# One layer with top-1 group, top-2 expert routing: expert weights with eight rows a partition, 2 MB requests, and router edits

## The reference

```python
x2 = x + g1 * rmsnorm(mixed)                      # residual after token mixing
h  = rmsnorm(x2, pre_ffn_gain) * (1 + sc2) + sh2
gl = h @ w_group + b_group                        # top-1 group, softmax probability
el = h @ w_expert + b_expert                      # top-2 experts inside that group
gates = one_hot(e_idx) * g_w * tv                 # 256 x 32, two nonzeros a row
for wg, wu, wd, gt in experts:                    # 1024x512, 1024x512, 512x1024
    hid = silu(h @ wg) * (h @ wu)
    out += gt[:, None] * (hid @ wd)
```

## Time and profile before

| | us |
|---|---|
| median of three runs | 647.47 |
| the profiled execution's own time | 648.19 |
| its span, first to last instruction | 646.5 |
| TensorE busy in the span | 613.5 (95%) |
| DMA moved | 248.71 MB, 385 GB/s over the span |

### The profile page before, as it was taken

One profiled execution on the slowest core, in us unless ns is written; L12 is line 12 of the kernel. 1 busy time (PEld: TensorE's weight loads), 2 busy tenths in 40 slices (PEclk: granted clock), 3 DMA queues, 4 the chain that ended last, 5 costly groups with the idle time before them and its releaser, 6 DMA issues.

```text
span 646.5 us, 8690 instructions
## 1 busy us (share of the span) xinstructions
PE 613.5 (95%) x3445; PEld 321.9 (50%) x3447; DVE 168.3 (26%) x317; ACT 143.4 (22%) x335; POOL 73.7 (11%) x161
## 2 busy tenths in 40 slices
PE   5999999999999999999999899999999999898984
PEld 5886687544664353543535355353543535344331
DVE  3644476970641110101101021010101101020104
ACT  4111334350532121221211122121221212112122
POOL 4700031020332110101101010010101101000000
PEclk9999999999879999999999999999999999999997
DMA  8999999699838999999999999999999999999981
GB/s 313 332 341 382 408 408 349 243 421 422 335 130 332 420 420 420 423 418 422 423 421 421 422 423 422 421 421 422 422 420 422 422 421 420 422 422 421 419 373 68
DMA packets 44747, 248.71 MB, mean 385 GB/s; under 512 B 5313, under 2 KB 5389, under 8 KB 18093
## 3 DMA queue, kind: packets, MB, share of 16 engines
q1 hardware_dynamic: 42304, 244.33, 92.9%
q0 software_dynamic: 944, 2.79, 1.2%
q10 hardware_dynamic: 1470, 1.22, 0.6%
...
## 4 chain that ended last, share of the span: by engine, by line
PE 60%; DMA 26%; issue 7%; DVE 2%; ACT 1%; POOL 1%; SPq 1%; DVEq 0%; ACTq 0%; POOLq 0%
PE PS L1622 26%; DMA W<-in_w_up_dram 20%; PE PS L1637 11%; PE PS L1552 5%; PE PS L1267 5%; DMA W<-in_w_in_dram 4%; PE PS L1594 3%; DMA W<-in_w_ada_dram 3%; PE PS L1438 2%; PE PS L1562 2%; PE PS L1652 1%; PE PS L1496 1%; PE PS L1220 1%; PE PS L1234 1%; PE PS L1277 1%
## 5 line engine op out<-in xcount | busy, mean ns | idle before, releaser
L1622 PE MATMUL PS<-W,XT 128*64 128x512 f32 x832 | 200.1, 595 | 9.0 <-DMA W<-in_w_up_dram 8.6
L1622 PEld LDWEIGHTS PS<-W,XT 128*64 128x64 f32 x832 | 64.3, 137 | 110.8 <-issue 108.1
L1136 DVE TENSOR_SCALAR XT<-PS,scol,shcol 128x128 f32<-128x128 f32 x64 | 21.8, 403 | 232.4 <-PE PS L1552 232.4
L1637 PE MATMUL PS<-V,HT 128*64 128x512 f32 x256 | 56.7, 595 | 1.5 <-DVE XT L1136 1.5
L1119 DVE SCALAR_TENSOR_TENSOR YL<-PS,gcol,YH 128x1024 fp32r<-128x1024 f32 x15 | 19.3, 1284 | 134.5 <-ACT YH L758 134.5
L1637 PE MATMUL PS<-W,HT 128*64 128x512 f32 x224 | 49.6, 595 | 0.0
L1552 PEld LDWEIGHTS PS<-OH,H 128*128 128x128 bf16 x768 | 43.5, 114 | 12.2 <-issue 12.2
L1552 PE MATMUL PS<-OH,H 128*128 128x128 bf16 x768 | 45.9, 220 | 0.0
L850 DVE SCALAR_TENSOR_TENSOR MOD<-W,cS,MOD 128x2048 f32<-128x2048 f32 x16 | 37.5, 2346 | 11.0 <-DMA W<-in_w_ada_dram 10.5
L758 ACT ACTIVATE YH<-PS,gcol 128x1024 fp32r<-128x1024 f32 x15 | 16.7, 1113 | 98.5 <-PE PS L1637 98.5
L1637 PEld LDWEIGHTS PS<-V,HT 128*64 128x64 f32 x256 | 18.2, 137 | 35.6 <-issue 35.6
...
## 6 DMA issues: line engine op xcount, KB each, us to landing
...
```

What stands on the lines that cost most here:

```text
L1136: nc.vector.tensor_scalar(XT[:, k, :], PS[:, 3, (k - 4) * P:(k - 3) * P], scol2[:, k:k + 1], shcol2[:, k:k + 1], ALU.mult, ALU.add).then_i ...
L1622: last = nc.tensor.matmul(PS[rows, u // 2, :], XT[:, k, rows], home(odd, unit_of(u, which), p)[:, q * FF:(q + 1) * FF], start=(k == 0), st ...
L1637: last = nc.tensor.matmul(PS[rows, 2 + q % 2, :], HT[:, k, rows], home(odd, unit_of(u, which), p)[:, q * FF:(q + 1) * FF], start=(k == 0), ...
```

## The change

1. Expert rows: partition p now has eight consecutive rows of a gate or up matrix (16 KB) and four of a down matrix (16 KB). A unit still is 8 KB a partition, the first or the second half of these. Tiles of two units (`WP`, `VP`) allow one request of 2 MB with 16 KB a partition for pairs (0,2), (4,6), (5,7), (8,10), (9,11) in turns 2 to 13 (not (0,2) in odd turns). Such a request waits for the later unit's user (`TAIL_OF`), and its one landing stands for both units.
2. `RUN_AHEAD` is 3: from turn 5 (and the rest of turn 4) requests go in order of need.
3. Last turn: units u = 3 and u = 5 are requested in halves of 0.5 MB, TensorE waits for each half; the scatter of the turn before goes ahead of u = 2; the last down takes its column groups in order.
4. H3 is stored in the order in which the gather reads it (contiguous 128 columns), so that ScalarE, VectorE and GpSimd write it (and GpSimd reads it) with a stride of 128 elements.
5. Router: GpSimd's L517 and L520 are gone, VectorE makes the rest of tokens 0 to 127 instead, ahead of the second half's; turn_over(2) before and after the second transposes; turn_over(9) for turn_over(4); ScalarE's transposed copy goes before its square root, and the copy of GU before the second exponential; router weights come in two requests and not four; adaLN columns are turned by eight transposes of 64 columns and not four of 128.

```diff
+HALVED = (3, 5)
 EVEN_OWN = (8, 9, 10, 11)
 ODD_OWN = (0, 1, 2)
 TWO_HOMES = ODD_OWN + EVEN_OWN
-RUN_AHEAD = 6
+RUN_AHEAD = 3
+TAIL_OF = {0: 2, 4: 6, 5: 7, 8: 10, 9: 11}
+JOINED = range(2, TURNS - 2)
...
-        W = [sb(f"W{slot}", [P, UW]) for slot in range(RING)]
+        WP = {v: sb(f"WP{v}", [P, 2 * UW]) for v in TAIL_OF}
+        W = [None] * RING
+        for head, tail in TAIL_OF.items():
+            W[slot_of(BASE + head)] = WP[head][:, 0:UW]
+            W[slot_of(BASE + tail)] = WP[head][:, UW:2 * UW]
+        for v in (1, 3):
+            W[slot_of(BASE + v)] = sb(f"WS{v}", [P, UW])[:]
...
-        V = [sb(f"V{n}", [P, UW]) for n in range(len(EVEN_OWN) + 1)]
+        VP = {v: sb(f"VP{v}", [P, 2 * UW]) for v in EVEN_OWN[0:2]}
+        V = [VP[v][:, 0:UW] for v in EVEN_OWN[0:2]] + [VP[v][:, UW:2 * UW] for v in EVEN_OWN[0:2]]
+        V += [sb("V4", [P, UW])[:]]
         H3 = sb("H3", [P, 3, TT, D], bf16)
         XT = sb("XT", [P, DC, 2 * SLOTS])
+
+        def in_rows(tile):
+
+            return tile.rearrange("p (d k) -> p d k", k=DC)
+
+        def part_rows(part, t):
+
+            return H3[:, part, t, :].rearrange("p (k d) -> p d k", k=DC)
...
+        def joined(turn, v):
+
+            return turn in JOINED and any(v in pair for pair in TAIL_OF.items()) and not (turn % 2 and v in ODD_OWN)
+
+        def landings(turn, v):
+
+            tails = tuple(TAIL_OF.values())
+            return sum(in_own(t % 2, v, 0) == in_own(turn % 2, v, 0) and not (v in tails and joined(t, v))
+                       for t in range(turn + 1))
+
         def unit_arrived(eng, i, odd, v, p):
 
-            if in_own(odd, v, p):
-                eng.wait_ge(own_in[v], i * 16 + 16)
-            elif p == 0 and v in TWO_HOMES:
-                eng.wait_ge(unit_in[slot_of(BASE + v)], i * 16 + 16 * uses_of(BASE + v))
-            else:
-                fills = uses_of(BASE + v) + odd + TURNS * p - (TURNS // 2 if v in TWO_HOMES else 0)
-                eng.wait_ge(unit_in[slot_of(BASE + v)], i * 32 + 16 * fills)
+            if p:
+                first = uses_of(BASE + v) - 1 + max(landings(TURNS - 2 + t, v) for t in range(2) if not in_own(t, v, 0))
+                eng.wait_ge(unit_in[slot_of(BASE + v)], i * 32 + 16 * (first + TURNS * (p - 1) + odd + 1))
+                return
+            before = 0 if in_own(odd, v, 0) else uses_of(BASE + v) - 1
+            if isinstance(i, int):
+                eng.wait_ge(landing(odd, v, 0), 16 * (before + landings(2 * i + odd, v)))
+                return
+            if joined(2 + odd, v) and v not in TAIL_OF:
+                v -= 2
+                before = 0 if in_own(odd, v, 0) else uses_of(BASE + v) - 1
+            first, step = landings(2 + odd, v), landings(4 + odd, v) - landings(2 + odd, v)
+            eng.wait_ge(landing(odd, v, 0), i * (16 * step) + 16 * (before + first - step))
+
+        def halves_arrived(eng, u, q, p):
+
+            for which in (0, 1):
+                if q == 0 and u in HALVED:
+                    eng.wait_ge(half_in[u][which], 16 * (p + 1))
+                elif q == (2 if u in HALVED else 0):
+                    unit_arrived(eng, LAST_TWO, 1, unit_of(u, which), p)
...
-                v = w.rearrange("l e (h p k) f -> h (l e) p (k f)", p=P, h=2)[u % 2]
+                v = w.rearrange("l e (p h k) f -> h (l e) p (k f)", p=P, h=2)[u % 2]
             else:
-                v = w_down.rearrange("l e (h p k) f -> h (l e) p (k f)", p=P, h=2)[u - 4]
+                v = w_down.rearrange("l e (p h k) f -> h (l e) p (k f)", p=P, h=2)[u - 4]
             return v[bass.ds(e, 1)].rearrange("a p f -> (a p) f")
+
+        def two_units_source(e, u):
+
+            w = (w_gate, w_up, w_down)[u // 2]
+            return w.rearrange("l e (p k) f -> (l e) p (k f)", p=P)[bass.ds(e, 1)].rearrange("a p f -> (a p) f")
...
+            def fetch_two(v, odd, e):
+                tile = VP[v] if in_own(odd, v, 0) else WP[v]
+                sp.dma_start(tile[:], two_units_source(e, v // 2)).then_inc(landing(odd, v, 0), 16)
...
+                if joined(turn, v) and v in TAIL_OF:
+                    return
                 sp.wait_ge(unit_used[v % 2], UPE * user + v // 2 + 1)
-                fetch(v, turn % 2, 2 * turn + v % 2)
+                if joined(turn, v):
+                    fetch_two(v - 2, turn % 2, 2 * turn + v % 2)
+                else:
+                    fetch(v, turn % 2, 2 * turn + v % 2)
+
+            def last_turn(p):
+
+                e = N_EXPERTS - 2
+                for u in range(UPE):
+                    halves = (slice(0, D), slice(D, 2 * D)) if u in HALVED else (slice(0, 2 * D),)
+                    for cols in halves:
+                        for which in (0, 1):
+                            v = unit_of(u, which)
+                            user = TURNS * (p + 1) - 1 - (2 if p == 0 and v in TWO_HOMES else 1)
+                            sp.wait_ge(unit_used[which], UPE * user + u + 1)
+                            sp.dma_start(home(1, v, p)[:, cols], unit_source(e + which, u)[:, cols]).then_inc(
+                                landing(1, v, p) if cols is halves[-1] else half_in[u][which], 16)
 
             def first_pass():
-                for v in range(UPT):
+                for v in (0, 1, 2, 3, 4, 5, 6, 7, 8, 10, 9, 11):
...
-                for turn in range(RUN_AHEAD + 2, TURNS):
+                for turn in range(RUN_AHEAD + 2, TURNS - 1):
                     for v in range(UPT):
                         load_unit(turn, v)
+                last_turn(0)
...
-            pool.wait_ge(stat_inv, 4)
-            nc.gpsimd.tensor_scalar(Hn[:, 0, :], X[:, 0, :], st[:, 51:52], None, ALU.mult).then_inc(h0_ready, 1)
-            pool.wait_ge(h0_ready, 1)
-            pool.wait_ge(high_ready, 1)
-            nc.gpsimd.tensor_tensor(Hn[:, 0, :], Hn[:, 0, :], H3[:, 0, 0, :], ALU.subtract).then_inc(rest_ready[0], 1)
             for t in range(TT):
                 pool.wait_ge(mid_ready, t + 1)
-                nc.gpsimd.tensor_tensor(H3[:, 2, t, :], Hn[:, t, :], H3[:, 1, t, :], ALU.subtract).then_inc(h3_ready, 1)
+                nc.gpsimd.tensor_tensor(part_rows(2, t), in_rows(Hn[:, t, :]), part_rows(1, t), ALU.subtract).then_inc(h3_ready, 1)
...
-            nc.scalar.copy(modR, PS[:, 4, :]).then_inc(strips_out, 1)
+            nc.scalar.copy(modR, PS[0:64, 4:6, :].rearrange("p b f -> p (b f)")).then_inc(strips_out, 1)
...
-            nc.scalar.mul(H3[:, 0, 0, :], X[:, 0, :], st[:, 51:52]).then_inc(high_ready, 1)
+            nc.scalar.mul(part_rows(0, 0), in_rows(X[:, 0, :]), st[:, 51:52]).then_inc(high_ready, 1)
...
+            x2_transposed(3)
             half_root(5, 2)
-            x2_transposed(3)
             act.wait_ge(rest_ready[0], 1)
-            nc.scalar.copy(H3[:, 1, 0, :], Hn[:, 0, :]).then_inc(mid_ready, 1)
+            nc.scalar.copy(part_rows(1, 0), in_rows(Hn[:, 0, :])).then_inc(mid_ready, 1)
             act.wait_ge(rest_ready[1], 1)
-            nc.scalar.copy(H3[:, 1, 1, :], Hn[:, 1, :]).then_inc(mid_ready, 1)
+            nc.scalar.copy(part_rows(1, 1), in_rows(Hn[:, 1, :])).then_inc(mid_ready, 1)
 
             act.wait_ge(group_sub, 1)
             nc.scalar.activation(rt[:, 0, :, 0:N_GROUPS], rt[:, 0, :, 0:N_GROUPS], ACT.Exp).then_inc(group_exp, 1)
+            act.wait_ge(mod_mm, 2)
+            nc.scalar.copy(GU[:], PS[:, 2:4, :].rearrange("p b f -> p (b f)")).then_inc(mod_row, 1)
             act.wait_ge(pair_sub, 1)
             nc.scalar.activation(st[:, 44:46], st[:, 44:46], ACT.Exp).then_inc(pair_exp, 1)
             nc.scalar.activation(st[:, 15:16], epsb[:], ACT.Silu).then_inc(warm, 1)
-            act.wait_ge(mod_mm, 2)
-            nc.scalar.copy(GU[:], PS[:, 2:4, :].rearrange("p b f -> p (b f)")).then_inc(mod_row, 1)
...
+            dve.wait_ge(high_ready, 1)
+            nc.vector.scalar_tensor_tensor(in_rows(Hn[:, 0, :]), in_rows(X[:, 0, :]), st[:, 51:52], part_rows(0, 0), ALU.mult, ALU.subtract).then_inc(rest_ready[0], 1)
             inverse(5)
             dve.wait_ge(stat_inv, 6)
-            nc.vector.tensor_scalar(H3[:, 0, 1, :], X[:, 1, :], st[:, 53:54], None, ALU.mult).then_inc(high_ready, 1)
+            nc.vector.tensor_scalar(part_rows(0, 1), in_rows(X[:, 1, :]), st[:, 53:54], None, ALU.mult).then_inc(high_ready, 1)
             dve.wait_ge(high_ready, 2)
-            nc.vector.scalar_tensor_tensor(Hn[:, 1, :], X[:, 1, :], st[:, 53:54], H3[:, 0, 1, :], ALU.mult, ALU.subtract).then_inc(rest_ready[1], 1)
+            nc.vector.scalar_tensor_tensor(in_rows(Hn[:, 1, :]), in_rows(X[:, 1, :]), st[:, 53:54], part_rows(0, 1), ALU.mult, ALU.subtract).then_inc(rest_ready[1], 1)
...
-                for q in range(4):
-                    last = nc.tensor.transpose(PS[:, 4, q * P:(q + 1) * P], modR[:, q:q + HALF - 3:4], ident[:])
+                for k in range(DC):
+                    last = nc.tensor.transpose(PS[:, 4, k * 64:(k + 1) * 64], modR[:, k:k + D - 7:8], ident[0:64, 0:64])
...
```

(28 more changed lines are left out.)

40 lines of the change are left out of this document (20 added, 20 removed).

## The result

The changed kernel takes 670.38 us (median of four runs, 668.69 to 676.76), the kernel before beside it 647.63. The ratio is 1.0368, with an interval of 1.0329 to 1.0407: **slower by 3.7%**, where 644.9 us was forecast. The profiled execution took 668.69 us with a span of 666.9, so 20.4 us more span than before.

The account below looks back on a forecast made before the run. The prediction took the stream of weights (full DMA engines) as the limit after the hole near 180 to 197 us. Its terms, -4.9 + 0.3 + 7.3 - 3.0 - 1.9 - 0.4 = -2.6, gave a median of 644.9 us, range 640.5 to 650.5.

Parts of the forecast that it names:

- Parts stored with strides: Router: VectorE's strided writes cost 0 to 0.8 us, taken as 0; those on ScalarE and GpSimd barely covered.
- Rival A: Router: GpSimd's low parts lock VectorE out of the choice; +2.3 to +7.3 us, 650 to 655; chance 0.20.
- Router -4.9: Router: without GpSimd's hold-up, no TensorE pause, full clock, faster logits; turn 0 starts earlier, 4.9 us saved.
- Requests +7.3: Weight stream: two-unit requests wait for the later user, so the stream stands still; 7.3 us lost in three stops.
- (a): Stop at the stream's restart, near 195 to 198 us: pair (0,2) waits for u = 1; idle 1.0 us.
- (b): Stop near 216 us: the first pair of down units waits for u = 5; idle 2.6 us.
- (c): Stop near 311 us, order of need: pair (4,6) waits for turn 4's u = 3; idle 3.7, single units nothing.
- Rate -3.0: Weight stream: 16 KB rows run at 427.5 GB/s for 421, saving 3.0 us over 80 of 108 paired units.
- Rival B: Weight stream: 16 KB rows gain no rate, 421 GB/s; +0.4 us or 647.9, no change; chance 0.17.
- C: Rival, weight stream: faster rate of 432 GB/s and no stop (c); 641 to 642 us; chance 0.15.
- D: Rival, weight stream: queued units cover stops (a) and (b); another 3 us, 642 us; chance 0.06.
- Last turn -1.9: Last turn: half-unit requests and the moved scatter shorten what follows the last landing by 1.9 us; zero if TensorE limits.

Follow-up runs that it names:

- e1: The changed kernel with H3 stored contiguously in row order as before, the gather reading weights with a stride of 8; 657.43 us, ratio 1.0149.
- g4: g3 with the change's strided stores of the parts, VectorE still making the low parts; 670.39 us, ratio 1.0336.
- g3: g2 with the change's requests for two units; 651.91 us, ratio 1.0089.
- e4: e1 with GpSimd's two low parts replaced by a memset of zeros; 655.35 us, ratio 1.0133.
- f1: The kernel before with the change's router edits alone, GpSimd still making the low parts; 649.26 us, ratio 1.0026.
- f2: f1 with both low parts on VectorE, GpSimd's G2*GU after the places, and 12 fillers for 9 behind the logits; 643.91 us, ratio 0.9950.
- g1: The kernel before with the edits of f2 and f3 together; 643.76 us, ratio 0.9930.
- g2: The changed kernel with contiguous stores, f2's low parts, every unit requested alone and RUN_AHEAD 6; 644.61 us, ratio 0.9948.
- f4: The kernel before with RUN_AHEAD 3 for 6 and nothing else; 649.95 us, ratio 1.0032.
- f3: The kernel before with the last turn's halves and turn 14's scatters ahead of u = 2; 646.97 us, ratio 0.9981.
- e2: e1 with every unit requested alone (JOINED empty); 655.14 us, ratio 1.0124.

## Why the prediction was wrong

**Parts stored with strides: the step that failed.** The text had "0 to 0.8 of cost, taken as 0" for VectorE and "Covered, barely" for ScalarE and GpSimd. It priced ScalarE's strided part at its contiguous time, without a bound, though no row of before showed such a store. The runs showed 4.85 to 5.02 us for 1.04 to 1.14 on ScalarE, 2.71 for 0.75 on VectorE and 4.8 to 5.0 for 2.1 on GpSimd (2.13 is e1's second low part). The first of these stands ahead of X on ScalarE, a queue that the sum never followed. It brings back the pause and the low clock (second transposes at 176.94 for 171.65, of which 1.7 is the late start of the router), and the middle parts push GpSimd onto the choice. In all some 13 us (change against e1), 18.5 where VectorE makes the low parts (g4 against g3). A rule that the prediction passed over stands in the Trainium skill, page "SBUF — State Buffer", section Door 1: The DMA port swizzle: each access that goes on to another 16-byte line pays a penalty. It gives no size. The traces agree that steps of 32 and of 256 bytes cost, and show what the rule doesn't say, that the one doubled ScalarE's time and the other took 4.3 to 4.8 times as long.

**Rival A, the lock, was true as a mechanism and had 0.20.** The sum put it at nothing on one row (L1008, two inputs of one element a partition, 0.16 us). That row is no counterexample: in e1 and the change two-input instructions of 4 to 32 elements wait for GpSimd's, TENSOR_REDUCE with one input doesn't, nor does anything wait for a memset. What makes L1008 different stays open. It is small, but also the GpSimd instruction around it (L517) has one tensor input, while each that held VectorE (L520, L589, L591) has two; and in the kernel before, at 17.29, six two-input instructions of VectorE (L867, 512 elements) beside GpSimd's one-input L471 (one element a partition) took 4.49 us together, 0.75 each as alone. It works the other way too: e1's first low part, begun beside L1100, took 2.98 us, the second 2.13. The page "SBUF — State Buffer" of the Trainium skill, section Who interferes with whom, says that the second of the two waits until the first is done, and e4, f1 and f2 agree with it, L1008 apart. The lock's price, with contiguous stores, is f1 against f2: 5.3 us. The rival's own start of turn 0, "0 to 5 us later than before", was too dear: with contiguous stores it is 0.9 later in f1 and 0.8 earlier in e1.

**Router -4.9: the mechanism held, where the parts allowed it.** L1023 without GpSimd beside it took 1.41 for two halves, the fillers bridged the pause, and the logits took 3.66 to 4.05 us. f2 gained 4.0 us. One thing the text had too simply: it tied the fall of the clock to a pause. In f2's trace the clock reads 0.62 at 176 to 178 and 0.53 at 178 to 180 with TensorE at work. In g1, whose router is the same, it stays at 1.00.

**Requests +7.3: right in kind, too small.** Measured in g3 against g2: (a) about 0.9 (1.0), (b) 2.1 (2.6), (c) 7.4 (3.7). In the change, (b) was 2.8 and (c) 6.6. Part of (c) is RUN_AHEAD's own: "With single units it would wait for u = 2 at 310.5, nothing" failed: f4, with single units and nothing else changed, lost 2.0 us. The sum looked at the request for the pair only. At the switch the stream also runs dry before unit 3's request (in g3 it moves 197 and 82 GB/s at 394 to 396). That the higher rate emptied the queue sooner and the earlier stops put TensorE later would explain it, but no run shows it by itself.

**Rate -3.0: right.** The line through the 2 KB and 8 KB rows gave 427.5 GB/s, and 426 to 428 was measured. g3's stops against g2 are 10.6 us (0.9, 2.1 and 7.4, and 0.2 at 200 to 210). By 620 its stream is 2.8 MB behind, or 6.6 us, so the rate gave back 4.0, which is 0.037 on each of the 108 units; the sum had counted 80 of them. At the last up product 7.9 us are left (617.20 against 625.10), because TensorE takes 1.3 back: after 563.72 it is the limit. Rival B falls with the rate, C and D with the stops.

**Last turn -1.9:** about -1.3 in f3, for the reason given as its bound: TensorE is the limit. The sum also had the last landing of before at 630.3, where in that trace the stream moves 238 GB/s at 628 to 629 and 25 in the next us, so the last down had more room than it thought. In the change TensorE is the limit from 580.75 on, for the last two turns, and halves of a unit have no landing to shorten. **Gather -0.4:** next to none. The weight load fell to 98 ns, but a gather at full clock went from 2.84 to 2.79 us only. **adaLN +0.3:** can't be told, since TensorE's arrival at the router varies by 2.5 us between e1 and e2, which have the same code up to there.

Between forecast and result lie 25.5 us: 13.0 of stores; 5.3 of the lock, which takes the router's gain away; 2.9 at (c) and 0.2 at (b), as the change has them; 0.6 at the last turn, 0.4 at the gather and 0.3 of rate, TensorE behind it included. That makes 22.7, and 2.8 are not assigned. The prices come from different kernels and need not add up: the stores alone cost 13.0 in one setting and 18.5 in another.

The theory of the experiments and its rival were both true in part: stores and lock are the larger share, and the requests with their order are a loss of their own, which the better rate doesn't pay for.
